# Transformer block, first part: the two longest blocks searched each by itself on ScalarE's counts, the embedding dealt in among the last counts

## The chip, the cores and the metric

One core of one Trainium2 chip. The metric is the device time of one execution in microseconds (us); lower is better. All times below are us from the start of the profiled span unless marked ns.

## The reference, cut to what matters

One transformer block over 2048 tokens of width 1024. Of its parts only the first matters here: the input projection, and for the sparse attention the choice of 256 keys for each token. For a block `j` of 128 tokens every key up to the token is scored, and the 256 best are kept, the earlier key where two are equal:

```python
def block(inp):
    j, qb, qib, wb = inp
    t_pos = j * Q_BLOCK + jnp.arange(Q_BLOCK)
    rel = jax.nn.relu(jnp.einsum('bthd,bsd->bths', qib, k_idx))
    score = jnp.einsum('bth,bths->bts', wb, rel).astype(f32)
    admissible = key_pos[None, :] <= t_pos[:, None]
    score = jnp.where(admissible[None], score, -jnp.inf)
    _, sel = lax.top_k(score, n_sel)
...
e = rms_norm(p[i] @ w_ple[i], g_ple[i])
h = h + e * jax.nn.sigmoid(h @ w_ple_gate[i])
```

The product `p @ w_ple` of the last two lines is the embedding; it depends on nothing else in the block, and the kernel computes it for the last seven token blocks at the end of its first part.

## The kernel before

The kernel runs in parts with a barrier of all engines between them; the first part is `project_and_select`. In it TensorE (PE) makes the input projection (`product`, in the trace L727 and L742), and between the products the index scores (`rel`, L757). ScalarE (ACT) copies products out of PSUM (`copy`), applies relu and weights to the scores (`relu_of`, `weigh`), and GpSimd (POOL) sums them and masks the diagonal of a finished block (L547, semaphore `S_masked`).

VectorE (DVE) searches, for each block from 2 to 15, the 256th largest score of each token, bit by bit: 31 bits, from the highest down, after a first count against zero. One bit is a **round**: for each block of a group one count of the scores at or above the trial value (L831, one pass over 128 x width, width 128 * (j + 1)), then a short instruction that tells whether the count is below 256 (`lower`, L857), and one that sets the next trial value (`flip`, L864). Groups are searched one after another: (2, 3), (4, 5), (6, 7), (8, 9, 10, 11), (12, 13, 14, 15). ScalarE helps: from bit 7 of the fourth group on and from bit 30 of the fifth it counts the last two blocks of the group as sums of signs (`sense`, L641), and VectorE turns each sum into a bit (L860) after its own two counts, so that the four blocks move on together. After the last bit comes `settle` for the two helped blocks (one more count each, L876, and a chain of 13 short integer instructions, L878 to L900). ScalarE then writes the side of each score against the value found (`tell`, L653), and VectorE picks (`pick`: L928, a running sum L930, L933, L935, and the mask itself L937). POOL stores each mask to DRAM (L577).

Every engine runs its own queue in order. The order of ScalarE's queue is made when the kernel is built, by a planner (`deal`): it walks through the work with constants for each step (`COUNT` is the fixed share of a count of VectorE) and puts a sense in front of the next copy or score piece when the sense is due no more than `LEAN` = 0.3 us after it. The planner only sets orders; waits are on semaphores.

After the products, and in ScalarE's queue after the last `tell`, comes the embedding, seven times: PE transposes a block of `p` (`turn_p`, L775), ScalarE copies it (`embed`, L677), PE multiplies (L784), ScalarE squares, copies and stores the result (`result`, L685, L687, L689). The first part is over when the last mask and the last embedding have landed in DRAM; the mixers (second part) begin behind the barrier.

## Time and profile before

| what | us |
|---|---|
| median of 3 runs (lowest, highest) | 2828.01 (2826.02, 2829.25) |
| the profiled execution, its own time | 2826.14 |
| its span | 2824.4 |
| first part, start of the span to the first work behind the barrier | 841.2 |

The profiled execution's time is 1.7 above its span, and 1.9 below the median of the runs. Busy time of an engine in a stretch, beside the stretch's length, tells how full it is; the timeline tells what stands in front of what.

### The profile page before, as it was taken

The numbers are of one execution on the slowest core, as the hardware profiler recorded it, in microseconds if no ns is written. First come the engines' busy times: TensorE is split into PE (matmuls) and PEld (weight loads), VectorE is DVE, ScalarE is ACT, GpSimd is POOL, SyncE is SP. The second block draws the span as 40 slices with busy tenths as digits, with TensorE's granted clock in tenths as the row PEclk, the third lists the DMA queues.
The fourth block names the chain that finished last, engine by engine and source line by source line (L and its number), as shares of the span: only waits on it lengthen the run. The fifth ranks groups of instructions, "written<-read, shape, count | busy, mean of one in ns | idle before, by whom it ended". The sixth has DMA issues, their size and how long they took to land. (4 is left out here: it accounts for less than half of the span.)

```text
span 2824.4 us, 35041 instructions
## 1 busy us (share of the span) xinstructions
PE 2588.1 (92%) x10908; PEld 1637.5 (58%) x10909; DVE 1860.8 (66%) x2646; ACT 1259.8 (45%) x2368; POOL 927.4 (33%) x925
## 2 busy tenths in 40 slices
PE   6999879999947889898899979999999999998998
PEld 3544424347823445444688756666666666665787
DVE  2389999979987788876333586644644444743676
ACT  2358667857956676766322222222222222222322
POOL 2377767810011111121000043434444444433221
PEclk9999989999967999999899989999999999999999
DMA  5202311122232223222544559975776665973663
GB/s 151 69 28 60 50 45 41 38 79 72 68 126 74 65 70 112 67 72 75 210 143 146 184 217 360 349 275 201 289 268 221 238 229 200 345 288 135 201 215 133
DMA packets 221475, 438.08 MB, mean 155 GB/s; under 512 B 22888, under 2 KB 91048, under 8 KB 221224
## 3 DMA queue, kind: packets, MB, share of 16 engines
q1 hardware_dynamic: 199400, 357.78, 36.9%
q0 software_dynamic: 13312, 47.32, 5.3%
q10 hardware_dynamic: 8640, 31.46, 2.8%
q8 instruction: 62, 1.02, 0.1%
q14 instruction: 61, 0.50, 0.1%
HBM read 331.14 MB, written 105.38 MB: 155 GB/s over the span
## 5 line engine op out<-in xcount | busy, mean ns | idle before, releaser
L2542 DVE CAST p_high<-p_low 128x2048 fp32r<-128x2048 f32 x128 | 203.2, 1587 | 400.8 <-PE p_psG L2649 293.0
L727 PE MATMUL p_psP<-home,p_ring 128*128 128x512 f32 x832 | 377.8, 604 | 11.3 <-DVE home L815 11.3
L2665 PE MATMUL p_psY<-p_wd,p_hT 128*128 x752 | 330.9, 593 | 2.2 <-ACT p_hT L2724 1.9
L2544 DVE TENSOR_TENSOR p_low<-p_low,p_high 128x2048 fp32r<-128x2048 f32 x128 | 318.9, 2492 | 4.4
L727 PEld LDWEIGHTS p_psP<-home,p_ring 128*128 128x128 f32 x832 | 153.8, 191 | 218.7 <-issue 206.1
L2665 PEld LDWEIGHTS p_psY<-p_wd,p_hT 128*128 128x128 f32 x752 | 139.3, 190 | 160.6 <-issue 160.5
L2585 POOL TENSOR_TENSOR p_xT_low<-p_xT,p_xT_high 128x512 fp32r<-128x512 f32 x94 | 186.0, 1997 | 3.3 <-ACT p_xT L2709 3.3
L2647 PE MATMUL p_psG<-p_high,p_xT_high 128*128 128x512 f32 x376 | 167.1, 444 | 15.7 <-DVE p_low L2544 8.0
L757 PE MATMUL p_psI<-p_kI,p_qI 64*128 64x512 f32 (+3 forms) x608 | 138.3, 574 | 27.7 <-ACT p_relu L618 26.2
L2591 POOL TENSOR_TENSOR p_hid<-p_act_g,p_act_u 128x512 f32<-128x512 f32 x47 | 62.1, 1321 | 308.2 <-ACT p_act_u L2719 295.3
L618 ACT ACTIVATE p_relu<-p_psI 128x1024 f32<-128x1024 f32 (+3 forms) x152 | 132.5, 914 | 64.3 <-PE p_psI L757 54.5
L2647 PE MATMUL p_psU<-p_high,p_xT_high 128*128 128x512 f32 x376 | 154.3, 410 | 5.6 <-DVE p_low L2544 5.6
L632 ACT ACTIVATE p_relu<-p_relu,p_small 128x512 f32<-128x512 f32 (+3 forms) x266 | 158.0, 664 | 0.0
L2730 ACT ACTIVATE p_y<-p_psY 128x512 f32<-128x512 f32 x94 | 56.2, 598 | 220.4 <-PE p_psY L2665 220.4
L2648 PE MATMUL p_psG<-p_low,p_xT_high 128*128 x376 | 150.3, 400 | 0.0
L2649 PE MATMUL p_psG<-p_high,p_xT_low 128*128 128x512 f32 x376 | 150.1, 399 | 0.0
L2648 PE MATMUL p_psU<-p_low,p_xT_high 128*128 x376 | 148.5, 395 | 0.0
L2649 PE MATMUL p_psU<-p_high,p_xT_low 128*128 128x512 f32 x376 | 148.5, 395 | 0.0
L2715 ACT ACTIVATE p_act_g<-p_psG 128x512 f32<-128x512 f32 x47 | 28.1, 598 | 261.9 <-PE p_psG L2649 261.9
L2719 ACT ACTIVATE p_act_u<-p_psU 128x512 f32<-128x512 f32 x47 | 28.1, 597 | 240.0 <-PE p_psU L2649 240.0
L641 ACT ACTIVATE p_rank<-p_S_high,p_flip 128x1920 uint8<-128x1920 f32 (+1 forms) x62 | 120.2, 1940 | 5.4 <-DVE p_flip L864 5.4
L757 PEld LDWEIGHTS p_psI<-p_kI,p_qI 64*128 64x128 f32 x608 | 53.0, 189 | 115.9 <-issue 81.1
(423 smaller groups left out, 5848.4 us busy)
## 6 DMA issues: line engine op xcount, KB each, us to landing
p_low<-in_w_expert_gate_dram SPq DMA_DIRECT2D x32, 2048.0 KB, 13.3
p_low<-in_w_expert_up_dram SPq DMA_DIRECT2D x32, 2048.0 KB, 18.1
p_wd<-in_w_expert_down_dram SPq DMA_DIRECT2D x32, 2048.0 KB, 10.7
y_dram<-p_y ACTq DMA_DIRECT2D x47, 512.0 KB, 7.9
p_xt<-in_x_dram SPq DMA_DIRECT2D x32, 512.0 KB, 4.6
y_dram<-p_clear SPq DMA_DIRECT2D x32, 512.0 KB, 4.4
proj_f<-p_stage SPq DMA_DIRECT2D x52, 256.0 KB, 2.4
p_ot<-o_dram SPq DMA_DIRECT2D x16, 512.0 KB, 4.3
```

The source lines that it names most:

```text
L618: act.activation(relu[:, n % NRELU, :, 0:c1 - c0], psI[:, n % NI, :, 0:c1 - c0], ACT.Relu).then_inc(relu_done, 1)
L632: act.activation(dst, src, ACT.Copy, scale=small[:, j, h:h + 1]).then_inc(weighed, 1)
L641: act.activation(sign_of[:, c, 0:width(j)], scores_of(S_low, S_high, j), ACT.Sign, scale=-1.0, bias=flip[:, own + c:own + c + 1].bitcast(F32),
L727: mm = pe.matmul(psP[0:n, i % 2, :], w, aT[:, k, c * CH:(c + 1) * CH], start=k == 0, stop=k == KD - 1)
L757: mm = pe.matmul(psI[:, n % NI, half, 0:c1 - c0], qI[r, b % 2, i, :], kI[r, c0:c1], start=True, stop=True)
L2542: dve.tensor_copy(high[:, m, k, :], low[:, par, m, k, :].bitcast(F32)).then_inc(high_done, 1)
L2544: dve.tensor_tensor(low[:, par, m, k, :], low[:, par, m, k, :].bitcast(F32), high[:, m, k, :].bitcast(F32), ALU.subtract).then_inc(w_split, 1)
L2585: pool.tensor_tensor(xT_low[:, k, :], xT[:, k, :], xT_high[:, k, :].bitcast(F32), ALU.subtract).then_inc(xT_split, 1)
L2647: pe.matmul(ps[:, :], xT_high[:, k, :], high[:, m, k, :], start=k == 0, stop=False)
L2648: pe.matmul(ps[:, :], xT_high[:, k, :], left, start=False, stop=False)
L2649: mm = pe.matmul(ps[:, :], xT_low[:, k, :], high[:, m, k, :], start=False, stop=k == KD - 1)
L2665: mm = pe.matmul(psY[:, c, :], hT[:, k, :], wd[:, bass.ds(at, 1), k, c * CH:(c + 1) * CH].rearrange("p a f -> p (a f)"), start=k == 0, sto ...
```

## The change

The two longest blocks, 14 and 15, leave the last group (`LONE`). Each is searched by itself: VectorE makes its first count (`lone_start`), ScalarE makes the count of every bit (`sense(c, b)`), and VectorE turns it into the next value with two short instructions, `lone_lower` and `lone_flip`, which the planner puts between two counts of a group, one of them for each block at each such place (`between`). The fourth group (8 to 11) is counted by VectorE alone in all rounds, and the fifth is (12, 13), VectorE alone. `settle` is made for blocks 14 and 15, each by itself; `tell` goes by group, and singly for 14 and 15. VectorE's queue is now planned too (`dve_order`). ScalarE's senses may start as soon as block 14 is masked. The embedding's steps are items P and E of the common order, so the planner may put senses and tells between them; the loads of its operands wait in SP's queue for the picks of blocks 8, 9 and 10, whose sides share the space. `COUNT` goes from 0.18 to 0.13. Small arrays get more columns, and the tables of position biases move to other partitions and are filled by POOL behind a wait for two masked blocks.

```diff
@@ -78,16 +78,17 @@
...
-GROUPS = [(2, 3), (4, 5), (6, 7), (8, 9, 10, 11), (12, 13, 14, 15)]
-GROUP_OF = {j: g for g, js in enumerate(GROUPS) for j in js}
+GROUPS = [(2, 3), (4, 5), (6, 7), (8, 9, 10, 11), (12, 13)]
+LONE = [14, 15]
+SIDE_IN = {12: 8, 13: 9, 14: 10, 15: 11}
...
-HELP_FROM = (-1, -1, -1, 7, 30)
-HELPED = (0, 0, 0, 2, 2)
-SEARCH_AT, LEAN, COUNT = 100.0, 0.3, 0.18
+PICKED = [j for js in GROUPS for j in js] + LONE
+TURN_LATE = 1
+SEARCH_AT, LEAN, COUNT = 100.0, 0.3, 0.13
...
@@ -196,9 +199,12 @@
         def side_of(j):
 
             if j >= LOW:
-                return scores_of(S_low, S_high, j - 4).bitcast(F16)[:, 0:width(j)]
+                return scores_of(S_low, S_high, SIDE_IN[j]).bitcast(F16)[:, 0:width(j)]
             return relu[:, :, :, :].rearrange("p b a n -> p (b a n)").bitcast(F16)[:, (j - 8) * 3 * CH:(j - 8) * 3 * CH + width(j)]
...
+        order += [("P", 0)]
+        for i in range(EARLY):
+            order += [("P", i + 1)] * (i + 1 < EARLY) + [("E", i)]
+        LAST_R = max(n for n, o in enumerate(order) if o[0] == "R")
...
+        TOLD = [js for js in GROUPS if js[0] >= MIDDLE] + [(j,) for j in LONE]
+        late = {j: i for i, j in enumerate(j for js in TOLD for j in js)}
+        LATE_PICKS = [j for j in PICKED if j >= MIDDLE and j not in LONE]
...
+            def between(t):
+
+                for c, j in enumerate(LONE):
+                    if c not in next_bit:
+                        if masked.get(j, 1e9) <= t:
+                            dve_out.append(("S", c))
+                            t += COUNT + 0.00104 * width(j) + 0.55
+                            next_bit[c] = NBITS - 1
+                            ready["C", (c, NBITS - 1)] = t + 0.1
+                    elif c in half_way:
+                        b = half_way.pop(c)
+                        dve_out.append(("F", (c, b)))
+                        t += 0.07
+                        if b > 0:
+                            ready["C", (c, b - 1)] = t + 0.1
+                        else:
+                            ended.add(c)
+                    elif sensed_at.get((c, next_bit[c]), 1e9) <= t:
+                        half_way[c] = next_bit[c]
+                        dve_out.append(("L", (c, next_bit[c])))
+                        next_bit[c] -= 1
+                        t += 0.07
+                return t
+
+            def picking(t, jj, js):
+                while js[0] >= MIDDLE and js[jj] not in told_at:
+                    yield None, t
+                dve_out.append(("K", (js, jj)))
+                W = width(js[jj])
+                yield True, max(t + 0.2 + 0.0026 * W, told_at[js[jj]]) + 1.2 + 0.00115 * W if js[0] >= MIDDLE else t + 0.9 + 0.00625 * W
...
+                    t = max([t] + [masked[j] for j in js])
+                    for b in range(NBITS, -1, -1):
+                        for jj, j in enumerate(js):
+                            yield True, t
+                            t = between(t)
+                            dve_out.append(("N", (g, b, jj)))
+                            t += COUNT + 0.00104 * width(j)
+                        dve_out.append(("B", (g, b)))
+                        t += 0.45
+                    if js[0] >= MIDDLE:
+                        ready["T", js] = t + 0.1
+                    for jj in range(len(js)):
+                        for go, t in picking(t, jj, js):
+                            yield go, t
+                        t = between(t)
+                for c, j in enumerate(LONE):
+                    while c not in ended:
+                        yield True, t
+                        t2 = between(t)
+                        if t2 == t:
+                            there = [sensed_at[k, b] for k, b in next_bit.items() if (k, b) in sensed_at] + [masked[k] for m, k in enumerate(LONE) if m not in next_bit and k in masked]
+                            if not there:
+                                yield None, t
+                            else:
+                                t2 = max(t, min(there))
+                        t = t2
+                    dve_out.append(("Z", c))
+                    t += COUNT + 0.00104 * width(j) + 2.3
+                    ready["T", (j,)] = t + 0.1
+                    for go, t in picking(t, 0, (j,)):
+                        yield go, t
+
...
+                item = 1e9
...
-                if max(ready, act_at) <= item + LEAN and ready < 1e9:
-                    g, b = ahead.pop(0)
-                    assert b >= 0 or all(kind != "R" for kind, _ in order[k:])
-                    act_at = max(act_at, ready) + 0.4 + sum((0.28 + 0.0008 * width(j)) for j in GROUPS[g][len(GROUPS[g]) - HELPED[g] if b >= 0 else 0:])
-                    counted[g, b] = act_at + 0.1
-                    out.append(("C", (g, b)))
+                let_dve(max(act_at, min(item, act_at + 3.0)))
+                allowed = [(t, w) for w, t in ready.items() if w[0] == "C" or k > LAST_R]
+                if allowed and max(min(allowed)[0], act_at) <= item + LEAN:
+                    t, what = min(allowed)
+                    del ready[what]
+                    act_at = max(act_at, t) + 0.05
+                    if what[0] == "C":
+                        act_at += 0.6 + 0.00077 * width(LONE[what[1][0]])
+                        sensed_at[what[1]] = act_at + 0.1
+                    else:
...
                 if i == len(products) - 8:
                     sp.wait_ge(rel_done, NREL)
                     sp.wait_ge(summed, NREL)
+                    sp.wait_ge(chosen, FREED)
                     sp.dma_start(wp, w_ple[0].rearrange("(k p) n -> p k n", p=P)).then_inc(p_loaded, 16)
...
+            def sense(c, b):
+
+                j, col = LONE[c], 4 + c
+                act.wait_ge(lone_flipped, flipped_by[c, b])
+                if sensed_by[c, b] > 0:
+                    act.wait_ge(sensed, sensed_by[c, b])
+                act.activation(sign_of[:, 0:width(j)], scores_of(S_low, S_high, j), ACT.Sign, scale=-1.0, bias=flip[:, col:col + 1].bitcast(F32),
+                               accum_out=signs[:, c:c + 1]).then_inc(sensed, 1)
+
+            def tell(js):
+
+                if js[0] in LONE:
+                    act.wait_ge(settled, LONE.index(js[0]) + 1)
                 else:
-                    act.wait_ge(mask_stored, 16 * (2 + LOW - MIDDLE))
-                for jj, j in enumerate(GROUPS[g]):
-                    act.activation(side_of(j), scores_of(S_low, S_high, j), ACT.Sign, scale=-1.0, bias=flip[:, jj:jj + 1].bitcast(F32),
-                                   accum_out=sums[:, jj:jj + 1]).then_inc(told, 1)
+                    act.wait_ge(flipped, (GROUPS.index(js) + 1) * (NBITS + 1))
+                for jj, j in enumerate(js):
+                    if j < LOW:
+                        act.wait_ge(summed, NREL)
...
-                if kind == "C" and i[1] < 0:
-                    tell(i[0])
+                if kind == "T":
+                    tell(i)
                 elif kind == "C":
                     sense(*i)
...
-            result(EARLY - 1)
+                elif kind == "P":
+                    embed(i)
+                elif kind == "E":
+                    result(i)
+
...
+                elif kind == "P":
+                    if i == 0:
+                        pe.wait_ge(copied, len(products))
+                        pe.wait_ge(p_loaded, 32)
+                        pe.wait_ge(relu_done, NREL)
+                    turn_p(i)
+                elif kind == "E":
+                    embed(i)
...
-                for b in range(NBITS - 1, -1, -1):
-                    own = n - HELPED[g] if (g, b) in sensed_by else n
-                    for jj, j in enumerate(GROUPS[g][0:own]):
-                        if jj >= 2:
-                            dve.wait_ge(step, steps - 1)
-                        at = chain(count(jj, j, flip[:, jj:jj + 1].bitcast(F32)))
...
-                    at = chain(dve.tensor_scalar(lower[:, 0:own], cnt[:, 0:own], float(TOPK), float(1 << b), ALU.is_lt, ALU.mult))
-                    for c in range(n - own):
-                        dve.wait_ge(sensed, sensed_by[g, b] + c + 1)
-                        at = chain(dve.tensor_scalar(lower[:, own + c:own + c + 1], signs[:, c:c + 1], float(width(GROUPS[g][own + c]) + 1 - 2 * TOPK), float(1 << b),
...
+            def lone_lower(c, b):
+
+                col = 4 + c
+                dve.wait_ge(sensed, sensed_by[c, b] + 1)
+                lowered[c] = chain(dve.tensor_scalar(lower[:, col:col + 1], signs[:, c:c + 1], float(width(LONE[c]) + 1 - 2 * TOPK), float(1 << b),
+                                                     ALU.is_gt, ALU.mult))
+
+            def lone_flip(c, b):
+
+                col = 4 + c
+                dve.wait_ge(step, lowered[c])
+                dve.scalar_tensor_tensor(out=flip[:, col:col + 1], in0=lower[:, col:col + 1], scalar=(1 << b) >> 1, in1=flip[:, col:col + 1],
+                                         op0=ALU.bitwise_xor, op1=ALU.bitwise_xor).then_inc(lone_flipped, 1)
+
...
+            def settle(c):
+
+                j, col = LONE[c], 4 + c
+                v, found = flip[:, col:col + 1], cnt[:, col:col + 1]
+                side, up, low, high, carried, change = (ints[:, i, :] for i in range(6))
+                dve.wait_ge(lone_flipped, flipped_by[c, -1])
+                count(col, j, v.bitcast(F32), ALU.is_gt)
...
+            for kind, i in dve_order:
+                if kind == "X":
                     turned_over(LAST_X, NT)
-                search(g)
-                if HELP_FROM[g] >= 0:
-                    settle(g)
-                    pick(g)
-                else:
-                    select(g)
+                elif kind == "N":
+                    count_bit(*i)
+                elif kind == "B":
+                    next_values(*i)
+                elif kind == "S":
+                    lone_start(i)
+                elif kind == "L":
+                    lone_lower(*i)
+                elif kind == "F":
+                    lone_flip(*i)
+                elif kind == "Z":
+                    settle(i)
+                elif kind == "K" and i[0][0] >= MIDDLE:
+                    pick(*i)
+                elif kind == "K":
+                    select(*i)
 
     return (kA, small), used
 
```

In the rest `count` takes the column and keeps account of which of the two scratch rows was last written, and `select` and `pick` take one block at a time, with the same instructions as before.

## Rows read from the trace of the kernel before

**Rows 1.** Busy time in two stretches; columns as the header line says.

```profile
500.00:600.00 100.00, 100.00 (x273) 40.61 (x272) 79.34 (x137) 78.17 (x111) 64.90 (x58) 1.00 0.14 45
...
750.00:800.00 50.00, 24.06 (x111) 20.48 (x109) 48.22 (x95) 39.60 (x46) 0.00 (x0) 0.75 0.42 130
```

**Rows 2.** Timeline, the last work of each engine in the first part.

```profile
829.34 2.35 DVE L937 SCALAR_TENSOR_TENSOR p_S_high<-p_rank,p_need,p_S_middle 128x2048 uint8<-128x2048 f16 x1
...
831.98 0.54 POOL L577 DMA_DIRECT2D mask_dram<-p_S_high  x1 [7.46 <-DVE p_S_high L937]
...
837.97 0.33 ACTq L689 DMA_DIRECT2D e_dram<-p_ring  x1
...
841.18 0.42 ACT L1413 ACTIVATE near<-near 128x256 f32<-128x256 f32 x1 [3.23 <-PEq L120]
```

**Rows 3.** DMA issues from 740 to 845: size, median us to landing.

```profile
e_dram<-p_ring ACTq DMA_DIRECT2D x7, 512.0 KB, 2.6
...
mask_dram<-p_S_high POOLq DMA_DIRECT2D x1, 256.0 KB, 2.4
```

**Rows 4.** Timeline of PE: the last products, then the embedding.

```profile
754.76 18.29 PE L742 MATMUL p_psP<-p_ring,home 128*128 128x256 f32 x84
...
807.88 6.15 PE L784 MATMUL p_psI<-p_kI,p_relu 128*128 128x512 f32 x8 [31.73 <-ACT p_relu L677]
```

**Rows 5.** Timeline of DVE: rounds of blocks 8 to 11, then what follows.

```profile
540.90 1.41 DVE L831 TENSOR_SCALAR_CACHE_REDUCE p_above<-p_S_middle,p_flip 128x1152 uint8<-128x1152 f32 x1
...
547.15 0.17 DVE L857 TENSOR_SCALAR p_psX<-p_cnt 128x4 int32<-128x4 f32 x1
...
547.55 1.41 DVE L831 TENSOR_SCALAR_CACHE_REDUCE p_above<-p_S_middle,p_flip 128x1152 uint8<-128x1152 f32 x1
...
560.86 1.41 DVE L831 TENSOR_SCALAR_CACHE_REDUCE p_above<-p_S_middle,p_flip 128x1152 uint8<-128x1152 f32 x1
...
575.39 0.16 DVE L860 TENSOR_SCALAR p_psX<-p_signs 128x1 int32<-128x1 f32 x1 [11.45 <-ACT p_rank L641]
...
608.57 1.68 DVE L876 TENSOR_SCALAR_CACHE_REDUCE p_above<-p_S_middle,p_flip 128x1408 uint8<-128x1408 f32 x1
...
614.24 0.82 DVE L928 TENSOR_SCALAR p_equal<-p_S_middle,p_flip 128x1152 uint8<-128x1152 f32 x1
...
638.39 1.89 DVE L831 TENSOR_SCALAR_CACHE_REDUCE p_above<-p_S_high 128x1664 uint8<-128x1664 f32 x1
```

**Rows 6.** Timeline of DVE: rounds of blocks 12 to 15, settling, first pick.

```profile
646.94 1.95 DVE L831 TENSOR_SCALAR_CACHE_REDUCE p_above<-p_S_high,p_flip 128x1664 uint8<-128x1664 f32 x1
...
757.03 1.95 DVE L831 TENSOR_SCALAR_CACHE_REDUCE p_above<-p_S_high,p_flip 128x1664 uint8<-128x1664 f32 x1
...
761.02 0.16 DVE L857 TENSOR_SCALAR p_psX<-p_cnt 128x2 int32<-128x2 f32 x1
...
761.10 0.21 DVE L860 TENSOR_SCALAR p_psX<-p_signs 128x1 int32<-128x1 f32 x2
...
793.37 2.21 DVE L876 TENSOR_SCALAR_CACHE_REDUCE p_above<-p_S_high,p_flip 128x1920 uint8<-128x1920 f32 x1
...
797.77 0.16 DVE L878 TENSOR_SCALAR p_ints<-p_flip 128x2 int32<-128x2 int32 x1
...
800.10 1.08 DVE L928 TENSOR_SCALAR p_equal<-p_S_high,p_flip 128x1664 uint8<-128x1664 f32 x1
```

**Rows 7.** Waits of DVE for ACT, from 100 to 600 and from 600 to 760.

```profile
DVE p_psX L860 <- ACT p_rank L641: 19.1, 6, 11.4
...
DVE p_psX L860 <- ACT p_rank L641: 5.2, 10, 1.8
```

**Rows 8.** Timeline of ACT: its count of block 15.

```profile
758.93 1.99 ACT L641 ACTIVATE p_rank<-p_S_high,p_flip 128x2048 uint8<-128x2048 f32 x1
```

**Rows 9.** Timeline of POOL: blocks 14 and 15 masked, the last two.

```profile
528.51 0.46 POOL L547 TENSOR_TENSOR p_S_high<-p_tri_big,p_S_high 128x128 f32<-128x128 f32 x1
...
573.43 0.46 POOL L547 TENSOR_TENSOR p_S_high<-p_tri_big,p_S_high 128x128 f32<-128x128 f32 x1
```

More of the change, by code:

```diff
@@ L343, in deal, with let_dve @@
+            program, over = on_dve(), False
+            def let_dve(until):
+                nonlocal dve_at, over
+                while not over and dve_at <= until:
+                    go, t = next(program, ("over", dve_at))
+                    dve_at = t
+                    if go == "over":
+                        over = True
+                    if go is None:
+                        return
+            k = 0
+            while k < len(order) or not over:
                 if k < len(order) and order[k][0] in "XQH":
@@ L758, in rel @@
                 mm.then_inc(rel_done, 1)
-            for kind, i in order:
-                if kind == "X":
-                    for t in range(i * TPC, (i + 1) * TPC):
-                        turn_x(t)
-                elif kind == "H":
-                    product(i, 0, KD // 2)
-                elif kind == "M":
-                    product(i, KD // 2 if ("H", i) in halved else 0)
-                elif kind == "R":
-                    rel(i)
             def turn_p(i):
@@ new lines, in count, with count_bit @@
+                which = 1 - which
+                if junk_used[which]:
+                    dve.wait_ge(step, junk_used[which])
+                junk_used[which] = chain(dve.tensor_scalar((above, equal)[which][:, 0:W], scores_of(S_low, S_high, j), value, None,
+                                                           compare, ALU.add, accum_out=cnt[:, col:col + 1]))
+                return junk_used[which]
+            counted = 0
+            turned_bits = 0
+            def count_bit(g, b, jj):
+                nonlocal counted
+                j = GROUPS[g][jj]
+                if b == NBITS:
+                    dve.wait_ge(S_masked, j - SCORED[0] + 1)
+                    counted = count(jj, j, 0.0)
+                else:
+                    counted = count(jj, j, flip[:, jj:jj + 1].bitcast(F32))
@@ new lines, in _, with lone_start @@
+            lowered = {}
+            def lone_start(c):
+                j, col = LONE[c], 4 + c
+                dve.wait_ge(S_masked, j - SCORED[0] + 1)
+                at = count(col, j, 0.0)
+                dve.wait_ge(step, at)
+                at = chain(dve.tensor_scalar(lower[:, col:col + 1], cnt[:, col:col + 1], float(TOPK), -1.0, ALU.is_lt, ALU.mult))
+                dve.wait_ge(step, at)
+                dve.tensor_scalar(flip[:, col:col + 1], lower[:, col:col + 1], 1 << (NBITS - 1), None, ALU.bitwise_xor).then_inc(lone_flipped, 1)
@@ new lines, in pick @@
+            def pick(js, jj):
+                nonlocal picked
+                j = js[jj]
+                col = 4 + LONE.index(j) if j in LONE else jj
+                W = width(j)
+                s = scores_of(S_low, S_high, j)
+                ties = equal[:, 0:W]
+                at = chain(dve.tensor_scalar(ties, s, flip[:, col:col + 1].bitcast(F32), None, ALU.is_equal))
+                dve.wait_ge(step, at)
+                at = chain(dve.tensor_tensor_scan(rank[:, 0:W], ties, ties, 0.0, ALU.add, ALU.bypass))
+                dve.wait_ge(step, at)
+                dve.wait_ge(told, late[j] + 1)
+                at = chain(dve.tensor_scalar(need[:, 0:1], rank[:, W - 1:W], sums[:, col:col + 1], 0.5, ALU.add, ALU.mult))
+                dve.wait_ge(step, at)
+                at = chain(dve.tensor_scalar(need[:, 1:2], need[:, 0:1], float(TOPK - W // 2), None, ALU.add))
+                dve.wait_ge(step, at)
+                picked += 1
+                dve.scalar_tensor_tensor(out=s.bitcast(U8)[:, 0:W], in0=rank[:, 0:W], scalar=need[:, 1:2], in1=side_of(j),
+                                         op0=ALU.is_le, op1=ALU.is_le).then_inc(chosen, 1)
+                dve.wait_ge(chosen, picked)
```

293 lines of the change are left out of this document (128 added, 165 removed).

## The prediction

> **What bounds the kernel now.** I read the first part by stretches, then the timeline of each engine up to the barrier, then the rounds of VectorE's search, then who waited for whom. In the stretch from 500 to 600 TensorE is busy all the time and ScalarE 78%; from 750 to 800 VectorE is busy 48.2 of 50 us and TensorE 24.1 [rows 1]. The products end at 773.1, and TensorE's first embedding product starts at 807.9, after 31.7 us of waiting [rows 4]: its operand is copied by ScalarE, whose queue has the search and the tells in front.
>
> The end of the part is a race of two tails [rows 2, 3]. VectorE ends its last mask at 829.34 + 2.35 = 831.7; POOL issues the store at 832.0 for 0.5, and it lands 2.4 later, at 834.9. ScalarE issues the last embedding store at 838.0 for 0.3, and it lands 2.6 later, at 840.9. The first work behind the barrier is at 841.2, that is 0.3 after the later one. So ScalarE's embedding sets the end, and VectorE's tail stands 6.0 us behind it: with the embedding out of the way, the first part would be over at 834.9 + 0.3 = 835.2, or VectorE's end plus 3.5. That 6.0 is all that the last step can give; from there every microsecond that the change puts on VectorE counts in full.
>
> **The change part by part, on VectorE.** Until block 14 is masked at 529 [rows 9] nothing that decides differs: the order of products and scores is the same, ScalarE had no senses there, and POOL's wait for two masked blocks is met as it stands behind both. From there I count what VectorE's queue gains and loses.
>
> *The fourth group, all four blocks in all rounds.* A round of four counts takes 547.55 - 540.90 = 6.65 [rows 5]. The last eight, shared with ScalarE, took 608.57 - 560.86 = 47.7; alone they take 8 x 6.65 = 53.2: **+5.5**. It is little, since VectorE waited 19.1 us for ScalarE in them, 11.4 at once [rows 5, 7].
>
> *Its settling goes*: 614.24 - 608.57 [rows 5]: **-5.7**.
>
> *First counts.* All four blocks of the fifth group have theirs in the round from 638.39 to 646.94, 8.55 [rows 5, 6]. After, 14 and 15 have their own, earlier, each with its own pair of short instructions, 0.40 as in 547.15 to 547.55: the same counts and two such pairs more: **+0.8**.
>
> *31 rounds of blocks 12 and 13.* Before: 793.37 - 646.94 = 146.4 [rows 6], in which 5.2 us of waits for ScalarE lie [rows 7]. A round without them: two counts, 761.02 - 757.03 = 3.99, and the pair, 0.40: 4.39; 31 of them are 136.1: **-10.3**.
>
> *The short instructions of 14 and 15*: 2 blocks x 31 bits x 2 = 124, between counts. No row shows one between two counts. The nearest: L860 starts 0.08 after L857 without waiting for it to end, and two of them take 0.21 together, so the second adds 0.06 [rows 6]. Alone one lasts 0.16 (L857, L878). I take 0.08: **+9.9**. The bounds are 124 x 0.065 = 8.1 and 124 x 0.16 = 19.8; nothing at all, if they hide under the start of the next count, stays as a case below.
>
> *Settling 14 and 15 one after the other.* Before 800.10 - 793.37 = 6.73, of which the integer chain is 800.10 - 797.77 = 2.33 [rows 6]. The chain is now made twice: **+2.3**. The picks keep their instructions, and a tell of 2.0 us [rows 8] is hidden behind the pick's running sum, as before.
>
> The sum is +5.5 - 5.7 + 0.8 - 10.3 + 9.9 + 2.3 = +2.5: VectorE ends at 834.2, the part at 837.7, which is 3.5 us earlier than 841.2. So the change doesn't unload VectorE. It exchanges 24.3 us of waits [rows 7] for 24.3 + 2.5 = 26.8 us of work of its own, and what it gains is the tail.
>
> **What hides the rest.** *The embedding.* From the first product at 807.9 to the last store at 838.3 seven blocks took 30.4, 4.3 each with the waits between TensorE and ScalarE [rows 2, 4]. They can begin when the products end, near 775, and have until 835. With one sense of 2.1 (below) in each, seven take 45 and end at 820; if that cover is gone the part ends as before. *The senses*: 62, of 2.0 to 2.1 us [rows 8], are 126 us. From 529 to 835 ScalarE also has scores until 574 (78% of 45 us, 35 [rows 1, 9]), eight tells of at most 2.0 (16) and at most 30 for the embedding: 207 of 306, and 99 are left for the copies of products. The load fits; the chain is the question, and it is the first rival. *SP and POOL*: the loads of `p` wait for picks that end near 640. They stand eight products before the end, near 745 (84 instructions take 18.3, so eight products of 16 take 28 [rows 4]); the stores of these eight, queued behind in SP, wait for nothing new. TensorE's products may slip when a copy stands behind a sense; they have some 15 us of room (835 against 820).
>
> Small stalls where the planned order meets real times (a sense behind a copy that waits for TensorE) cost 5.2 us in the fifth group before [rows 7]. Now the value is asked for at a place where the planner had it finished, so I take 1 us, between 0 and 5.2: the gain is 2.5 us.
>
> **The rivals.** *First: the chain of block 15 ends too late* (slower). A block by itself moves only where VectorE passes between two counts: one place to lower, the next to flip, then a sense of 2.1 plus about 0.3 of hand-over. In the fifth group places lie 1.9 apart and then 2.4 (two counts in 4.39, plus short ones), so one block alone makes one bit in a round of 4.7. Two blocks need 4.1 of ScalarE in 4.7 and miss the place by 0.1, so together they make about 1.5 bits. In the fourth group's rounds (6.65, some 6.9 with the additions) a bit takes three places of four, two blocks some 2.2 bits a round. While the scores run, ScalarE has 22% free [rows 1]: some 4 bits for block 14 until 573.9, when 15 is masked [rows 9]. Then about 6 rounds with 14 bits until 621, and 4 in the places behind the four picks: 22 of 62 are done at 646, 40 are left. The fifth group has 32 rounds, and I need 28 to 31. The last of them meet the embedding on ScalarE. So the chain ends just at the end of the rounds, and the two picks absorb one more bit. A bit left after them costs its sense and hand-over bare, 2.6 us, since VectorE has nothing else. It decides from the fourth: 4 bits left are -2.5 + 10.4 = +7.9, 2836. For it: the margin is a tenth of the rounds. Against: a real round of two counts takes 4.39, the planner's constants make it 4.30, and this gives the senses time. Up to three bits stay within my forecast.
>
> *Second: the short instructions pay their whole length* (slower). Then 124 x 0.16 = 19.8, the part ends 9.9 later than in my sum: +7.4, 2835.5. L857 and L860 overlapping [rows 6] speak against it; that none of the rows stands between two long counts speaks for it. The Trainium skill (VectorE: DVE Perf Modes, "The DRAIN you can't avoid") says that the next operation does not start until the pipe is empty, and that this holds with or without semaphores; by that rule this rival is the case. The same page excepts an instruction that is not held, and with the exception it is my forecast.
>
> *Third: they cost nothing* (faster). The read of the accumulator already overlaps the next count; if a short one does too, 9.9 less: -12.4, 2815.6. L860 adding 0.06 to 0.08 even behind another short one [rows 6] speaks against it.
>
> *Fourth: the change doesn't do what it says*, the embedding still ends last. If products slip and the steps of embedding line up behind senses and tells, the last store stays near 838 and the part near 841: 2828.
>
> **How the numbers follow.** My forecast 0.54; the first rival 0.25; the second 0.06; the third 0.07; the fourth 0.08. The median of the runs is 1.9 above the profiled execution's time, and the sum is a difference, so I put it on the median: 2828.0 - 2.5 = 2825.5. My forecast's own range is 2822.5 (short instructions at 0.065, no stall) to 2833.3 (three bits, +5.3). The range over the cases is 2819 to 2838: below it lies the third rival, above it a chain late by more than four bits. 0.2% is 5.7 us, about what a measurement of this kernel can tell from no change. VectorE's sum can hardly give more than the 6.0 of the tail less 0.8, so faster by more is the third rival and a remainder of 0.05: 0.12. Slower by more is the first two and a little of the three-bit edge, 0.31. The rest, 0.57, is no change.
>
> **What the changed profile would show.** The last store of the embedding lies tens of us ahead of the last mask, and the work behind the barrier starts 3.5 after VectorE's last pick (the tail). Rounds of the fourth group stay at 6.65 plus 0.08 for each short instruction, those of the fifth near 4.7. VectorE's waits for ScalarE are near 1 us instead of 24. The two settlings are 4.5 and 4.6. What would make me wrong: VectorE idle before L or F between the pick of 13 and the settling of 14 or 15, a pitch of short instructions away from 0.08, or scores that slip because senses of block 14 stand in front of them, so that block 15 is masked later than about 577.

## The result and the profile after

The changed kernel takes 2833.37 us (median of 16 runs, 2830.46 to 2836.90), the one before 2826.56 (16 runs beside them): ratio 1.0023, 95% interval 1.0016 to 1.0031. It is slower by 6.8 us. I had forecast 2825.5 and no change.

The profiled executions are 2836.10 (after) and 2826.14 (before), 10.0 apart. Of these, 6.9 lie in the first part, which the rest of this text is about; the other 3 lie behind the barrier. In the profiles of all fourteen kernels the stretch behind the barrier takes between 1982.8 and 1986.3 us, with no order by kernel that I can see. So that 6.9 agrees so well with 6.8 is in part chance.

The part that I had not looked at gives it away. Timelines of GpSimd from 137 us, while it fills the bias tables; before the change first, then after. The last row of each is the first instruction behind the fill.

```profile
139.39 0.41 POOL L559 MEMSET p_rows_a<- 4x384 f32 x1
...
140.27 0.31 POOL L566 TENSOR_SCALAR p_rows_a<-p_raw_a 4x1 f32<-4x1 f32 x1
140.54 0.18 POOL L568 COPY p_rows_s<-p_raw_s 8x1 f32<-8x1 f32 x1
140.71 0.27 POOL L566 TENSOR_SCALAR p_rows_a<-p_raw_a 4x1 f32<-4x1 f32 x1
...
153.16 0.30 POOL L513 TENSOR_SCALAR p_small<-p_small 128x32 f32<-128x32 f32 x1
```

```profile
139.26 0.41 POOL L641 MEMSET p_rows<- 4x384 f32 x1
...
140.25 0.31 POOL L648 TENSOR_SCALAR p_rows<-p_raw 4x1 f32<-4x1 f32 x1
140.62 0.18 POOL L650 COPY p_rows<-p_raw 8x1 f32<-8x1 f32 x1
140.90 0.27 POOL L648 TENSOR_SCALAR p_rows<-p_raw 4x1 f32<-4x1 f32 x1
...
160.24 0.30 POOL L594 TENSOR_SCALAR p_small<-p_small 128x32 f32<-128x32 f32 x1
```

Each instruction is as long as before (0.27 and 0.18), but they start farther apart. The 32 pairs take 160.24 - 140.25 = 19.99 instead of 153.16 - 140.27 = 12.89: 7.1 us more, or 0.11 for each change from one table to the other. Behind the fill in GpSimd's queue stands the scaling of the weights (`weigh_ready`), and ScalarE and all scores wait for it. ScalarE's timeline, the first weighing of block 4, before and after:

```profile
153.49 0.72 ACT L632 ACTIVATE near<-p_relu,p_small 128x512 f32<-128x512 f32 x1 [1.79 <-POOL p_small L513]
```

```profile
160.57 0.72 ACT L718 ACTIVATE near<-p_relu,p_small 128x512 f32<-128x512 f32 x1 [8.99 <-POOL p_small L594]
```

The slip grows on its way. TensorE's timeline over the same pieces, before and after:

```profile
154.14 1.35 PE L757 MATMUL p_psI<-p_kI,p_qI 64*128 64x512 f32 x8
155.42 3.70 PE L727 MATMUL p_psP<-home,p_ring 128*128 128x512 f32 x8
```

```profile
155.29 3.70 PE L816 MATMUL p_psP<-home,p_ring 128*128 128x512 f32 x8
165.88 2.50 PE L846 MATMUL p_psI<-p_kI,p_qI 64*128 64x512 f32 x8 [6.88 <-ACT p_relu L704]
168.31 5.05 PE L816 MATMUL p_psP<-home,p_ring 128*128 128x512 f32 x8
```

Before, TensorE had no gap here. Now it stands for 6.9 of the 7.1 us, because ScalarE has not emptied its PSUM buffers, and works slower when it starts again: 2.50 and 5.05 us for what took 1.35 and 3.70, 2.5 us more. The granted clock is 0.50 (the level of 1.2 GHz) from 166 to 170 and back at 1.00 (2.4 GHz) from 174. POOL masks block 4 at 181.88 instead of 171.93, 10.0 us late.

From there everything slides. VectorE's start of the fourth group, before and after; the second row of each is the first round with trial values:

```profile
401.42 1.35 DVE L831 TENSOR_SCALAR_CACHE_REDUCE p_above<-p_S_middle 128x1152 uint8<-128x1152 f32 x1 [0.46 <-POOL p_S_middle L547]
407.83 1.41 DVE L831 TENSOR_SCALAR_CACHE_REDUCE p_above<-p_S_middle,p_flip 128x1152 uint8<-128x1152 f32 x1
```

```profile
409.14 1.35 DVE L926 TENSOR_SCALAR_CACHE_REDUCE p_equal<-p_S_middle 128x1152 uint8<-128x1152 f32 x1
...
415.51 1.75 DVE L926 TENSOR_SCALAR_CACHE_REDUCE p_above<-p_S_middle 128x1536 uint8<-128x1536 f32 x1 [2.06 <-POOL p_S_middle L628]
...
417.70 1.41 DVE L926 TENSOR_SCALAR_CACHE_REDUCE p_equal<-p_S_middle,p_flip 128x1152 uint8<-128x1152 f32 x1
```

The slip is 417.70 - 407.83 = 9.9 us. Of it 7.7 lie in the start of the group (409.14 against 401.42) and 2.1 in a wait for block 11 ahead of its first count; more on that wait below. The masks of blocks 14 and 15 come 12.1 and 13.4 later than in [rows 9]:

```profile
540.61 0.46 POOL L628 TENSOR_TENSOR p_S_high<-p_tri_big,p_S_high 128x128 f32<-128x128 f32 x1
...
586.83 0.46 POOL L628 TENSOR_TENSOR p_S_high<-p_tri_big,p_S_high 128x128 f32<-128x128 f32 x1
```

Now the place where I expected trouble. First VectorE's timeline within the rounds of blocks 12 and 13 (against [rows 6]), the settling of block 15, and the last mask; then the ends of ScalarE and GpSimd, against [rows 2].

```profile
742.29 0.16 DVE L976 TENSOR_SCALAR p_psX<-p_signs 128x1 int32<-128x1 f32 x1
742.36 1.94 DVE L926 TENSOR_SCALAR_CACHE_REDUCE p_equal<-p_S_high,p_flip 128x1664 uint8<-128x1664 f32 x1
744.22 0.08 DVE L926 DVE_READ_ACCUMULATOR p_equal<-p_S_high,p_flip 128x1 f32 x1
744.22 0.16 DVE L976 TENSOR_SCALAR p_psX<-p_signs 128x1 int32<-128x1 f32 x1
744.29 0.15 DVE L983 SCALAR_TENSOR_TENSOR p_flip<-p_psX,p_flip 128x1 int32<-128x1 int32 x1
744.35 2.07 DVE L926 TENSOR_SCALAR_CACHE_REDUCE p_above<-p_S_high,p_flip 128x1792 uint8<-128x1792 f32 x1
...
829.30 2.35 DVE L926 TENSOR_SCALAR_CACHE_REDUCE p_above<-p_S_high,p_flip 128x2048 uint8<-128x2048 f32 x1
...
833.80 1.28 DVE L1048 TENSOR_SCALAR p_equal<-p_S_high,p_flip 128x2048 uint8<-128x2048 f32 x1
...
840.01 2.35 DVE L1058 SCALAR_TENSOR_TENSOR p_S_high<-p_rank,p_need,p_S_middle 128x2048 uint8<-128x2048 f16 x1
848.05 0.23 DVE L1798 TENSOR_TENSOR p_both<-ident 128x64 f32<-128x64 f32 x1 [5.69 <-PEq L121]
```

```profile
827.11 0.33 ACTq L762 DMA_DIRECT2D e_dram<-p_ring  x1
```

```profile
842.66 0.54 POOL L661 DMA_DIRECT2D mask_dram<-p_S_high  x1 [12.56 <-DVE p_S_high L1058]
```

A short instruction between two counts costs 0.07 (742.29 to 742.36, 744.22, 744.29, 744.35); the embedding's last store is out 15 us ahead of the last mask's. Waits of VectorE from 380 to 850, and of ScalarE from 540 to 850, against [rows 7]; the columns are us in total, times and the longest:

```profile
DVE p_need L1053 <- ACT p_S_middle L743: 0.8, 1, 0.8
```

```profile
ACT p_sign_of L726 <- DVE p_flip L983: 54.5, 40, 4.3
```

VectorE has no wait for ScalarE left but 0.8 us; ScalarE is the one that waits. The search works as I had it, only late. The first work behind the barrier comes 848.05 - 841.18 = 6.9 us later: 9.9 of slip, +0.8 that VectorE's own work from 417.70 on is longer (424.66 against 831.69 - 407.83 = 423.86), and 5.7 from the last pick to the first work where 9.5 stood: -3.8.

### The profile page after: what moved, and what is told of

Same layout as the page of the kernel before. It is cut to its first block and busy times, and to the rows that moved or that the text cites. A ratio compares the mean times of both kernels' runs of the same rounds, so it can differ in the third digit from the quotient of the medians.

```text
span 2834.3 us, 35278 instructions
## 1 busy us (share of the span) xinstructions
PE 2597.2 (92%) x10908; PEld 1641.3 (58%) x10909; DVE 1883.8 (66%) x2724; ACT 1238.0 (44%) x2336; POOL 928.9 (33%) x925
## 5 line engine op out<-in xcount | busy, mean ns | idle before, releaser
L726 ACT ACTIVATE p_sign_of<-p_S_high,p_flip 128x1920 uint8<-128x1920 f32 (+1 forms) x62 | 120.8, 1948 | 56.3 <-DVE p_flip L983 54.5
L1663 PE MATMUL p_psX<-p_kA,near 64*128 64x512 f32 (+3 forms) x320 | 86.4, 619 | 42.8 <-ACT near L1544 31.6
```

The source lines that it names most:

```text
L726: act.activation(sign_of[:, 0:width(j)], scores_of(S_low, S_high, j), ACT.Sign, scale=-1.0, bias=flip[:, col:col + 1].bitcast(F32), accum_ ...
```

## The experiments

What I had to settle: does the fill cost the time (theory A) or the search itself (B), and is it the alternation, or the merged tile (C)? Twelve kernels ran, in three lots, each lot beside runs of the kernel before on the same chip. Every ratio below is against the kernel before in the same lot. Its median was 2824.77 in the first lot (both tables at 0, in turn, merged tables, fill ahead of the wait), 2825.55 in the second (embedding last, last mask's store, tables at block 4, three lone blocks) and 2827.79 in the third (own tiles, the two runs in which ScalarE waits, tables at block 8). So runs of different lots are compared by their ratios, or by the times in their profiles. "In turn" below means this edit of the changed kernel, nothing else:

```diff
             for b, lo, hi in bucket_ranges():
...
                 pool.tensor_scalar(rows_a[:, at], ...)
+            for b, lo, hi in bucket_ranges():
...
                 pool.tensor_copy(rows_s[:, at], ...)
```

**Both tables at partition 0 again.**

```diff
-        raw, rows_of = sb("raw", [32 + SH, NB_BUCKETS]), sb("rows", [32 + SH, 384])
...
+        raw_a, raw_s = sb("raw_a", [AH, NB_BUCKETS]), sb("raw_s", [SH, NB_BUCKETS])
+        rows_a = sb("rows_a", [AH, 384])
+        rows_s = sign_of[0:SH, 0:384 * 4].bitcast(F32)
...
+                if sensed_by[c, b] == 0:
+                    act.wait_ge(rows_stored, 32)
```

> The changed kernel, but both bias tables start at partition 0 again, as before the change: the first one's rows and the two raw tables have tiles of their own, the second one's rows borrow the bytes of the tile that ScalarE's lone counts write from 550 us on (ScalarE waits once for the store of the tables before its first lone count). Theory A (what slows the change is GpSimd's fill of the tables, whose 32 pairs take 0.60 to 0.67 us each instead of 0.37 since the two tables start at different partitions): the fill takes 14 us again instead of 21.0, the first round of blocks 8 to 11 starts at about 400 to 402 instead of 409.1, and the kernel takes 2823 to 2827 us, 6 to 10 less than the changed one. Theory B (the new order of the search itself costs the time: the fourth group's counts, the short instructions, the later end of VectorE): 2832 to 2834. If A holds only in part (the fill mended, but the wait for the tables' store at 340 to 378 us stays 3.7 longer): 2827 to 2830.

Measured: 2824.74, the kernel before 2824.77, ratio 0.9997 (0.9988 to 1.0006). The 6.8 us are gone. Theory A; B is out.

**In turn.**

> The changed kernel with its merged tables at partitions 0 and 32, but GpSimd fills the whole of one table and then the whole of the other, instead of one entry of each in turn. Theory A as alternation (an instruction costs more when it starts at other partitions than the one before it): the fill takes 12 to 14 us, 2824 to 2828 us in all. Theory C (partition 32, or the merged tile, is slow by itself): the second table's entries stay slow, the fill takes 17 to 21 us and the kernel 2829 to 2834. Theory B: 2832 to 2834 whatever the fill takes.

Measured: 2823.45, ratio 0.9996 (0.9987 to 1.0005). The same tiles, the same partitions, one change between them. GpSimd's timeline of this run:

```profile
139.99 8.78 POOL L648 TENSOR_SCALAR p_rows<-p_raw 4x1 f32<-4x1 f32 x32
148.83 4.00 POOL L653 COPY p_rows<-p_raw 8x1 f32<-8x1 f32 x32
152.92 0.30 POOL L594 TENSOR_SCALAR p_small<-p_small 128x32 f32<-128x32 f32 x1
```

The 64 instructions take 12.9 us, as before the change, and the entries at partition 32 are the quick ones: 0.125 each. So partition 32 is not slow. The waits that the change adds to the fill are still there, so it is not they either.

**The kernel before with merged tables, filled alternately** (the tiles of the change, its waits, nothing of its search).

> The kernel before the change, with that one part of it alone: the bias tables in merged tiles at partitions 0 and 32, filled alternately, with the waits that go with it. Theory A: the fill takes 21 us, block 8 to 11 are masked 8 to 14 us later, and the kernel takes 2833 to 2837 us, 7 to 10 more than before. Theory B: the fill takes 21 us, but blocks 8 to 15 wait for something else anyway, and the kernel takes 2826 to 2828.

Measured: 2834.79, ratio 1.0036 (1.0022 to 1.0050): 10.0 us more. Block 4 is masked at 180.7, and TensorE stands for 6.9 us and then takes 2.50 and 4.88 as above. In the changed kernel the same slip is worth 8.1 (6.8 above the kernel before with it, 1.3 below with the tables in turn), 10.5 in the profiles; here it is 10.0 and 8.7. The search makes no clear difference to it.

**Own tiles, two start partitions.**

```diff
-        raw, rows_of = sb("raw", [32 + SH, NB_BUCKETS]), sb("rows", [32 + SH, 384])
...
+        raw_a, rows_a = sb("raw_a", [AH, NB_BUCKETS]), sb("rows_a", [AH, 384])
+        rows_s = sign_of[32:32 + SH, 0:384 * 4].bitcast(F32)
+        raw_s = sign_of[32:32 + SH, 384 * 4:(384 + NB_BUCKETS) * 4].bitcast(F32)
...
```

> The changed kernel with the tables filled in turn entry by entry, as the change has it, in four tiles of their own (one pair inside the tile of the lone counts), the first pair starting at partition 0 and the second at 32. It tells the start partition from the sharing of a tile. Theory A (alternating start partitions cost GpSimd about 0.11 us at each switch): the fill takes 21 us again, 2832 to 2835 us. Theory C (what costs is that both tables lie in one tile): 14 us, 2823 to 2826 us.

Measured: 2832.54, ratio 1.0017 (1.0007 to 1.0026), 4.8 us more than the kernel before. That is 2 less than the changed kernel's 6.8; the fill tells more. GpSimd's timeline:

```profile
140.18 0.32 POOL L648 TENSOR_SCALAR p_rows_a<-p_raw_a 4x1 f32<-4x1 f32 x1
140.56 0.18 POOL L650 COPY p_sign_of<-p_sign_of 8x1 f32<-8x1 f32 x1
140.84 0.27 POOL L648 TENSOR_SCALAR p_rows_a<-p_raw_a 4x1 f32<-4x1 f32 x1
...
160.13 0.30 POOL L594 TENSOR_SCALAR p_small<-p_small 128x32 f32<-128x32 f32 x1
```

19.95 us for the 32 pairs, with nothing shared between the first table's tiles and the second's. Theory C is out: it is the change of the start partition. Only the starts 0 and 32 were tried.

**In turn, and the fill ahead of GpSimd's wait for the index queries.**

> As the run with the tables filled one after the other, and the fill moved ahead of GpSimd's wait of 16.6 us for the stores of the index queries (121 to 138 us), into which it then falls. Theory A: the 12 to 14 us leave the way of block 4's scores; ScalarE waited only 1.8 us for them in the kernel before, so 1 to 3 us more come off than in the run without the move: 2821 to 2826 us. If GpSimd's later work had no slack at all before the change either, up to 14 us come off: 2812. Theory B: 2832 to 2834.

Measured: 2823.93, ratio 0.9997 (0.9988 to 1.0006). The fill ended at 134.5 and the weights were ready at 145.7, 7 us earlier than in turn alone, but block 4 was masked at 171.1 against 171.7: GpSimd only waited longer, 6.9 us, for ScalarE's copy of the weights. TensorE has no gap there in this run, nor in the kernel before, so ScalarE's wait of 1.8 us was not on the path, and taking the fill of 13.8 us away gains nothing that shows. The path came close behind it, though: of the 7.1 us that alternating adds, TensorE lost 6.9.

**The embedding last again, in turn.**

```diff
+        act_order = [o for o in act_order if o[0] not in "PE"] + [o for o in act_order if o[0] in "PE"]
```

> The changed kernel with the tables filled one after the other, but all seven embedding tiles again behind ScalarE's last telling, as in the kernel before. It prices the part of the change that puts the embedding among the last counts. From rows: block 15 is told at about 825.5, seven tiles at 3.66 to 4.3 us of TensorE follow, the last store at about 855 and the first work behind it at 857 to 858 instead of 837.5: 19 to 21 us more, 2842 to 2845 us. Rival (ScalarE's waits had hidden it anyway, and the end is VectorE's): 2823 to 2826.

Measured: 2844.44, ratio 1.0066 (1.0051 to 1.0082), first work at 858.6, 21.0 more than in turn. So with this search the early embedding is needed: block 15 is told at 823 instead of 805.5, and an embedding behind that ends later. The reverse, the embedding moved and the old search kept, was not run.

**The last mask's store from ScalarE's queue, in turn.**

```diff
             for n, j in enumerate(PICKED):
+                if j == PICKED[-1]:
+                    continue
...
+            act.wait_ge(chosen, len(PICKED))
+            act.dma_start(mask_dram[NT - 1, :, 0:L], ...).then_inc(lone_stored[-1], 16)
```

> The changed kernel with the tables filled one after the other, and the last mask's store (block 15) issued from ScalarE's queue instead of GpSimd's. In the run without this edit VectorE's last pick ended at 831.86 and the first work behind the barrier came at 837.54, 5.7 us later (my prediction had 3.5 for it); an embedding store issued from ScalarE's queue let the next part go 3.2 us after its issue. Theory A (GpSimd's queue is the slow piece of that tail): 3.3 to 3.7 us from pick to first work, 2 us less, 2821 to 2822. Rival (the mask's 256 KB in pieces of 2 KB need the time in any queue): no change, 2823 to 2825.

Measured: 2823.95, ratio 0.9995 (0.9986 to 1.0004). VectorE's timeline, then ScalarE's:

```profile
830.36 2.35 DVE L1065 SCALAR_TENSOR_TENSOR p_S_high<-p_rank,p_need,p_S_middle 128x2048 uint8<-128x2048 f16 x1
837.76 0.23 DVE L1805 TENSOR_TENSOR p_both<-ident 128x64 f32<-128x64 f32 x1 [5.05 <-PEq L121]
```

```profile
832.74 0.33 ACTq L791 DMA_DIRECT2D mask_dram<-p_S_high  x1
```

The store landed 2.0 us after its issue, at 834.7, and yet the next part began at 837.8. The queue was worth 0.6 of the 2 I expected; the other 3 us lie behind the landing. GpSimd still waited for it.

**The same, and ScalarE waits for the store instead of GpSimd.**

```diff
-            for c in range(len(LONE)):
+            for c in range(len(LONE) - 1):
                 pool.wait_ge(lone_stored[c], 16)
...
+            act.wait_ge(lone_stored[-1], 16)
```

> The changed kernel with the tables filled one after the other, the last mask's store issued from ScalarE's queue, and ScalarE instead of GpSimd waiting for it: against the run without the last edit (pick ended at 832.71, store issued 832.74, landed at about 834.7, first work 837.74) it tells only who waits. Theory A (GpSimd's way from its last wait to the barrier costs 2.3 us more): first work 2.6 to 2.9 us behind the end of the pick instead of 5.0, 2821 to 2823 us. Rival: no change, 5.0 and 2823 to 2825.

Measured: 2821.84, ratio 0.9979 (0.9970 to 0.9988).

```profile
829.50 2.35 DVE L1066 SCALAR_TENSOR_TENSOR p_S_high<-p_rank,p_need,p_S_middle 128x2048 uint8<-128x2048 f16 x1
834.38 0.23 DVE L1806 TENSOR_TENSOR p_both<-ident 128x64 f32<-128x64 f32 x1 [2.52 <-PEq L121]
```

From the pick's end to the first work 2.5 us instead of 5.0, and only the engine that waits was changed. In the kernel before this was hidden: its last mask was out 6 us before the embedding.

**The tables stored from ScalarE's queue at block 4, in turn.**

> The changed kernel with the tables filled one after the other, and the broadcast store of both bias tables (2.36 MB) issued from ScalarE's queue when block 4 is weighed (about 155 us), instead of from SyncE's queue ahead of the first later product, where ScalarE waits 25 to 28 us for the stage stores behind it. Theory A: that wait goes, block 11 is masked at about 375 instead of 404 us, but VectorE comes to the fourth group only at about 402, so its rounds start 2 us earlier at most and the kernel takes 2820 to 2824; ScalarE's copies and the embedding end 20 us earlier in idle time. Rival (the store collides with the loads of this stage, where it now falls): block 4 to 7 are masked later and the time rises to 2826 to 2832.

Measured: 2836.14, ratio 1.0039 (1.0025 to 1.0052). 10.6 us more than the kernel before: the direction of the rival, beyond its range, and for another reason than a collision. ScalarE's timeline:

```profile
152.58 12.16 ACTq L713 DMA_DIRECT2D bias_rows<-p_rows  x2
164.78 0.72 ACT L721 ACTIVATE near<-p_relu,p_small 128x512 f32<-128x512 f32 x1 [14.07 <-issue]
```

To issue the two broadcast stores holds ScalarE's own queue for 12.2 us, and block 4 was masked at 186.2 instead of 171.7. TensorE stood for 12.0 us and worked slower behind it here too. Block 11 came at 385 instead of 404, as theory A had it, and it helped nothing.

**Three lone blocks, and VectorE takes lone counts itself when it has nothing else** (with the last mask's store from ScalarE's queue, in turn).

```diff
-GROUPS = [(2, 3), (4, 5), (6, 7), (8, 9, 10, 11), (12, 13)]
-LONE = [14, 15]
+GROUPS = [(2, 3), (4, 5), (6, 7), (8, 9, 10, 11), (12,)]
+LONE = [13, 14, 15]
...
+                            free = [(ready["C", (m, b)], m, b) for m, b in next_bit.items() if ready.get(("C", (m, b)), 1e9) <= t]
+                            if free:
+                                _, m, b = max(free, key=lambda f: f[2])
+                                dve_out.append(("D", (m, b)))
...
```

> As the run with the last mask's store on ScalarE's queue, and the search dealt anew: block 13 is searched by itself too (62 counts of VectorE's 1.95 us leave its rounds, 31 of them for good), and VectorE, once blocks 12's rounds are over and nothing told by ScalarE is there to be taken up, makes 12 of the lone counts itself. In the changed kernel ScalarE waited 54.5 us for VectorE's values while VectorE waited for nothing, so VectorE alone set the end. Theory A (the whole part is now bounded by VectorE's work up to 832, and work moved to ScalarE's idle time comes off in full): the last pick ends 15 to 20 us earlier, 2803 to 2809 us. Rival (ScalarE becomes the bound: its counts push the last products and the embedding back): the embedding ends past 835, 2820 to 2830 us.

Measured: 2807.05, ratio 0.9933 (0.9919 to 0.9946). The last pick ended at 812.5, 19.4 earlier, ScalarE's wait for VectorE's values fell from 54.8 us (in turn) to 20.8, and ScalarE issued its last embedding store at 813.4: the two engines now end together. The trace has the 12 lone counts on VectorE. The edit also changes constants of the planner and which sense it takes first, and no run tells how much of the gain comes from the third lone block, the shared counts or the order.

**The same with ScalarE waiting for the last store.**

> As the run with three lone blocks, shared counts and the last mask's store on ScalarE's queue, but ScalarE waits for the landing of that store and GpSimd does not. In that run the store had landed at about 816.8 and the first work behind the barrier came at 819.7; where an embedding store is the last thing waited for, by ScalarE, 0.6 us lie between landing and first work. Theory A (GpSimd needs some 2.3 us more than ScalarE from its last wait to the barrier, which is the 2.2 us that my prediction's tail lacked): first work at 817.4, 2804 to 2806 in all, 2 us less. Rival (the landing itself is what counts): no change, 2806 to 2808.

Measured: 2803.99, ratio 0.9915 (0.9901 to 0.9928), 23.8 us less than the kernel before, and below the changed kernel too (2833.37, from another lot). First work at 817.4, as expected: 2.3 us less. The ratio alone would say 5 us, but the two runs are of different lots.

**The same with the tables' store in ScalarE's queue at block 8.**

> As the run before this one in the list, with the broadcast store of the tables issued from ScalarE's queue when block 8 is weighed (about 250 us), and ScalarE's and VectorE's work dealt for that. Issued at block 4 it held block 4 up by 14 us and everything behind it, but took away the wait of 27 us at 340 to 367 us. Theory A (VectorE works without a stop from 247 to 402 us, so 14 us more for blocks 8 to 10 are hidden, and ScalarE's later work comes 13 us earlier and finds room for more counts): 2796 to 2804 us. Rival (the place of the store moves no end that counts, and its delay reaches block 11 or 15): 2806 to 2815.

Measured: 2803.54, ratio 0.9913 (0.9900 to 0.9927), no different from the run before. Block 8 was masked 14.5 us later, block 11 1.5 earlier, the first work came at 817.6. The time lies in theory A's range, but only because that of the run before does; the mechanism is the rival's first half, the store's place moves no end that counts.

## Why the prediction was wrong, point by point

*"Until block 14 is masked at 529 nothing that decides differs."* This is the step that failed and made the result. I had read the order of products and scores, the senses and the added wait, but not the partitions: the tables' move from partition 0 to 0 and 32 gave GpSimd 63 changes of start partition at 0.11 us each, 7.1 us in a queue that ScalarE was already waiting for by 1.8. TensorE stood for 6.9 of them and lost another 2.5 at half clock. The first round of the fourth group came 9.9 late, and the whole 6.8 us of the result is undone by filling the tables in turn (2823.45 beside 2824.77).

*VectorE's sum.* Right in its parts. Rounds of four stay at 6.65, the settlings are 4.5 (833.80 - 829.30) and 4.4 against 4.6 and 4.5, the stall is 0.8 against 1. The term most off is the 124 short instructions: 0.07, not 0.08, 8.7 us instead of 9.9. In the run in turn VectorE's work from its first round of trial values to its last pick takes 831.86 - 407.11 = 424.75, 0.9 more than before, against +2.5 forecast; 1.2 of the difference are the short instructions.

*The tail.* Mis-sized: from pick to first work 5.7, not 3.5. The landing times of [rows 3] count from the start of the issue, so my sum had the issue in twice: the embedding landed at 840.6, 0.6 ahead of the first work, and the mask's tail would have been 3.3. The rest is another engine's doing. I had added the landing of a mask's store to what follows an embedding's store, and missed that GpSimd, once it is the last to wait, brings some 2.5 us of its own to the barrier. In sum the run in turn has its first work at 837.5, which is 3.6 earlier than before, where my sum, less its 1 us of stall, said 3.5; VectorE's sum 1.6 too high and its start 0.7 earlier cancel the 2.2 of the tail. That three errors cancel to 0.1 us is luck, the more so as the two profiles are of different lots. Its time of 2823.45 beside 2824.77 agrees with the 2.5 us forecast and can't be told from nothing.

*The rivals.* The chain of block 15 was not late, but just in time, as I had counted: in the run in turn 22 of the 62 senses have started by 646, and block 15 gets its last value at 787.99, 2.6 us ahead of the first pick; ScalarE's 54.5 us of waits are for the places that VectorE gives it. The short instructions at whole length are out: 0.07 where each lasts 0.16, between two counts of 2 us. The Trainium skill (VectorE: DVE Perf Modes, "The DRAIN you can't avoid") would go with that rival where it says that the next operation does not start until the pipe is empty; its exception for an instruction that is not held agrees with the rows. At nothing they are out too. The embedding no longer ends last, and the run with it at the end prices that half at 21 us.

The time lay in the range, on the side that I gave 0.31, by a mechanism that was in none of my cases: that it fell inside is luck.

What stays open: with the new search, ScalarE's wait for the stage stores at 340 to 367 us is 27.4 to 28.9 in all kernels where it stands, and 24.7 and 24.9 in the kernel before and the one with merged tables. It makes block 11 some 4 us late (404.4 in turn against 400.6) and costs VectorE a wait of 2.1 instead of 0.5. In the two runs with the tables' store in ScalarE's queue the wait is gone, so that store is its cause; why it lasts 3 us longer with the new search, no run tells.

## What to carry to other kernels

In a diff that says it is about one stage, cost the lines about memory layout too, and ask of each what order of instructions runs over it: the part of the change that decided was a tile of 40 partitions in place of two. An engine that another already waits for, be it by 2 us, has next to no slack: of 7.1 us lost there TensorE lost 6.9, and 2.5 more at the lower clock. That does not turn round: taking the whole fill out of the way gained nothing. When one engine never waits and another waits 54 us for it, the next step is to move work between them, and here it gave 17 us (2823.95 to 2807.05 in one lot) where the change's own sum had 2.5. Let the engine with the shortest way to the barrier wait for the last store.

## What the runs showed of the hardware

- GpSimd pays for a change of start partition between neighbouring instructions: 0.11 us each, with instructions of 0.18 and 0.27 and the starts 0 and 32. The Trainium skill (GPSIMD Engine Reference, "Instruction dispatch") says that each core serves 16 partitions of every instruction and starts the next when its own share is done. By that I would have looked for overlap between tables at partitions 0 and 32; the rows show the reverse: 20.0 us instead of 12.9.
- Who waits last matters: from the landing of a store to the first work behind the barrier some 3 us when GpSimd waits for it (834.7 to 837.7), 0.5 to 0.6 when ScalarE does (816.9 to 817.4, and in the kernel before 840.6 to 841.2).
- The issue of a broadcast store of 2.36 MB from 4 and 8 partitions holds ScalarE's queue for 12.2 us. A mask of 256 KB landed 2.4 us after its issue from GpSimd's queue, 2.0 from ScalarE's, and 2.9 there right behind an embedding's store.
- A short instruction between two long counts of VectorE starts together with the read of the count's accumulator (both at 744.22) and delays the next count by 0.07.
- TensorE, at a granted clock of 1.00 before, stood for 6.9 us and started again at 0.50: the same 8 matmuls took 2.50 instead of 1.35, the next 8 took 5.05 instead of 3.70. Three other runs with such a gap, of 6.8 to 12.0 us, show 2.50 or 2.51 and then 4.29 to 4.88.
